# Index scores on 64 rows instead of 128, two heads side by side, issued between the token blocks of a weight phase

## The reference, cut to what matters

```python
def dsa_attention(h, w_in, q_gain, k_gain, w_uv, w_out, rel_bias):
    topk = min(TOPK_MAX, S // 4)
    q, lat, qi, ki, wi = jnp.split(h @ w_in, [o1, o2, o3, o4], axis=-1)
    q = rms_norm(q.reshape(B, S, DSA_HEADS, DSA_LATENT), q_gain)
    k = rms_norm(lat, k_gain)
    vals = lat
    qi = qi.reshape(B, S, IDX_HEADS, IDX_DIM)
    wi = wi * (IDX_HEADS ** -0.5)
    # for each block of 128 queries at t:
        isc = relu(einsum('bqhd,bsd->bqhs', qi_block, ki))      # one key row for all 8 heads
        isc = einsum('bqhs,bqh->bqs', isc, wi_block)
        isc = where(key_pos <= t, isc, NEG_2)
        _, sel = top_k(isc, topk)
        # softmax attention of the 16 heads over the selected keys, with a bias by distance
```

## Time and profile before

| | |
|---|---|
| runs before | 2037.31, 2037.4, 2040.08 us; median 2037.4 us |
| profiled execution | 2039.25 us; span of its instructions 2037.5 us |
| the stretch from the first index score to the last copy before the attention | about 1405 to 1524 us of the span |
| ACT busy over the span | 560.5 us (28%) |
| POOL busy over the span | 1215.8 us (60%) |
| chain that ended last, by engine | PE 90%, DVE 6%, ACT 2% |

### The profile page before, as it was taken

The page is one execution under the profiler, slowest core; times in us unless marked ns, Lnnn a source line. Parts: engine busy times, 40 slices in busy tenths (PEclk is TensorE's granted clock), DMA queues, the critical chain, the costliest instruction groups (busy, mean ns, idle before and its releaser), DMA issues.

```text
span 2037.5 us, 26586 instructions
## 1 busy us (share of the span) xinstructions
PE 1952.1 (96%) x9256; PEld 1570.0 (77%) x9264; DVE 1071.3 (53%) x1655; ACT 560.5 (28%) x1107; POOL 1215.8 (60%) x683
## 2 busy tenths in 40 slices
PE   6989999999998899998999999999999999999999
PEld 4876788888887777786788888877776678888887
DVE  4366479787785704555434433143986554333422
ACT  3117220000114306563312111132446522121110
POOL 6660578887674565566566666646660058666664
PEclk9999999999998899999999999999999999999999
DMA  6440267776551131114233233213220013332231
GB/s 246 134 162 5 63 206 258 247 238 219 192 169 58 63 103 42 42 42 160 68 105 101 93 97 99 93 52 104 73 83 2 1 62 114 93 100 95 93 101 64
DMA packets 62181, 221.14 MB, mean 109 GB/s; under 512 B 6763, under 2 KB 7019, under 8 KB 61980
## 3 DMA queue, kind: packets, MB, share of 16 engines
q1 hardware_dynamic: 44928, 161.25, 24.7%
q10 hardware_dynamic: 17180, 58.92, 8.1%
HBM read 218.00 MB, written 2.14 MB: 108 GB/s over the span
## 4 chain that ended last, share of the span: by engine, by line
PE 90%; DVE 6%; ACT 2%; issue 1%; DMA 1%; POOL 0%; ACTq 0%; DVEq 0%; SPq 0%
PE bank L300 25%; PE bank L302 24%; PE bank L301 24%; PE bank L330 2%; PE bank L795 2%; PE bank L335 2%; PE bank L331 2%; PE bank L413 1%; DVE y L1643 1%; PE bank L618 1%; PE bank L754 1%; PE bank L630 1%; PE bank L805 1%; PE bank L643 1%; PE bank L1257 1%
## 5 line engine op out<-in xcount | busy, mean ns | idle before, releaser
L1111 POOL TENSOR_TENSOR w_lo<-raw,w_hi 128x1024 fp32r<-128x1024 f32 (+1 forms) x305 | 771.2, 2529 | 25.0
L300 PE MATMUL bank<-a_hi,w_hi 128*128 128x512 f32 x1960 | 767.0, 391 | 7.2 <-ACT big L1346 3.5
L302 PE MATMUL bank<-a_hi,w_lo 128*128 128x512 f32 x1960 | 764.6, 390 | 0.0
L301 PE MATMUL bank<-a_lo,w_hi 128*128 128x512 f32 x1960 | 764.6, 390 | 0.0
L1106 POOL TENSOR_SCALAR w_hi<-raw 128x1024 fp32r<-128x1024 f32 x299 | 351.2, 1175 | 587.2 <-PE bank L302 362.9
L300 PEld LDWEIGHTS bank<-a_hi,w_hi 128*128 128x128 f32 x1960 | 369.0, 188 | 85.8 <-ACT big L1346 4.8
L302 PEld LDWEIGHTS bank<-a_hi,w_lo 128*128 128x128 f32 x1960 | 369.1, 188 | 77.3
L301 PEld LDWEIGHTS bank<-a_lo,w_hi 128*128 128x128 f32 x1960 | 369.1, 188 | 76.3
L1643 DVE CUSTOM_DVE_ANT_0 y<-y,cond 128x1024 f32<-128x1024 f32 x96 | 221.7, 2347 | 3.3 <-DMA y<-in_ada 3.3
L1658 DVE SCALAR_TENSOR_TENSOR tmp<-bank,vecs,tmp 128x511 f32<-128x511 f32 x88 | 66.0, 750 | 262.7 <-ACT tmp L1364 262.7
L1364 ACT ACTIVATE tmp<-bank,vecs 128x512 f32<-128x512 f32 x88 | 68.7, 782 | 372.6 <-PE bank L302 364.7
(11 more groups left out here) (232 smaller groups left out, 2140.4 us busy)
## 6 DMA issues: line engine op xcount, KB each, us to landing
raw<-in_stream SPq DMA_DIRECT2D x299, 512.0 KB, 3.5
y<-in_ada ACTq DMA_DIRECT2D x96, 512.0 KB, 4.6
x<-in_x SPq DMA_DIRECT2D x4, 512.0 KB, 7.0
bias<-in_bias ACTq DMA_DIRECT2D x1, 2048.0 KB, 14.1
y<-rel_rows ACTq DMA_DIRECT2D x1, 2048.0 KB, 8.8
bias<-rel_rows ACTq DMA_DIRECT2D x1, 2048.0 KB, 17.4
out<-x SPq DMA_DIRECT2D x8, 256.0 KB, 2.0
cond<-in_c ACTq DMA_DIRECT2D x1, 512.0 KB, 9.2
```

The lines of the kernel that those rows point to most:

```text
L300: pe.matmul(o, lhs_hi, rhs_hi, start=start, stop=False, **kw)
L301: pe.matmul(o, lhs_hi, rhs_lo, start=False, stop=False, **kw)
L302: return pe.matmul(o, lhs_lo, rhs_hi, start=False, stop=stop, **kw)
L1111: m = pool.tensor_tensor(w_lo[:, s, part], raw[:, j, part], f32(w_hi[:, s, part]), ALU.subtract)
```

## The change

Three things are done at once. Each head's matmul contracts over its own 64 rows (`half(h)`), so that the zeroed halves of `tmp` and the two memsets that made them are gone; the two heads of a pair are issued one right behind the other, on the upper and lower 64 rows, into two banks. The unit of issue is now a pair (12 in all), and the pair waits once, for both relus of the pair before it. Pairs are issued inside the dq blocks 1 to 6, behind token tiles 1 and 3 of each. Last, ACT's queue is rearranged to suit: relus 0 to 11, the copies of group 0, relus 12 to 15, and then two relus behind each token tile of squares.

```diff
-            def index_scores(n):
-                i, h = 1 + n // IDX_HEADS, n % IDX_HEADS
-                cols = P * (i + 1)
-                if n == 0:
+            def index_scores(pair):
+                if pair == 0:
                     pe.wait_ge(*freed("ki", 1))
-                    pe.wait_ge(index_init, 8)
+                    pe.wait_ge(index_init, 6)
                     pe.wait_ge(wi_taken, 1)
-                if n >= 2:
-                    pe.wait_ge(relu_ready, n - 1)
-                pe.matmul(bank[(4, 6)[n % 2]][:, 0:cols], big[:, 16 + h // 2, i * P:(i + 1) * P], tmp[:, 2 + h % 2, 0:cols],
-                          start=True, stop=True).then_inc(index_ready, 1)
+                else:
+                    pe.wait_ge(relu_ready, 2 * pair)
+                for n in (2 * pair, 2 * pair + 1):
+                    i, h = 1 + n // IDX_HEADS, n % IDX_HEADS
+                    cols = P * (i + 1)
+                    pe.matmul(bank[(4, 6)[n % 2]][:, 0:cols], big[half(h), 16 + h // 2, i * P:(i + 1) * P],
+                              tmp[half(h), 2 + h % 2, 0:cols], start=True, stop=True).then_inc(index_ready, 1)
...
-                m.then_inc(block_done, 1)
+                    if t == TT - 1:
+                        m.then_inc(block_done, 1)
+                    if t % 2 and i and 2 * (i - 1) + t // 2 < 3 * IDX_HEADS // 2:
+                        index_scores(2 * (i - 1) + t // 2)
...
-                for n in {0: range(6), 1: range(6, 12), 2: range(12, 18), 5: range(18, 24)}.get(i, ()):
-                    index_scores(n)
...
-            for n in range(18):
+            for n in range(12):
                 index_relu(n)
             token_copies(0)
+            for n in range(12, 16):
+                index_relu(n)
             a.wait_ge(lat_summed, 1)
             for t in range(TT):
                 token_squares(0, t)
-            for n in range(18, 3 * IDX_HEADS):
-                index_relu(n)
+                for n in range(16 + 2 * t, 18 + 2 * t):
+                    index_relu(n)
...
-            v.memset(tmp[64:P, 2, :], 0.0).then_inc(index_init, 1)
-            v.memset(tmp[0:64, 3, :], 0.0).then_inc(index_init, 1)
```

More of the change, by code:

```diff
@@ L1861, in index_add @@
                     v.wait_ge(wi_taken, 1)
-                    v.wait_ge(index_init, 8)
+                    v.wait_ge(index_init, 6)
                 else:
```

## The result

Over 18 runs each, the changed kernel took 2042.17 us (2040.68 to 2043.74) and the kernel before 2038.92 us: a ratio of 1.0016 with a 95% interval of 1.0009 to 1.0023, so 3.2 us slower. The prediction of 2036.9 us was wrong: the time lies above its range of 2033.2 to 2040.8, and half a microsecond less was forecast where three more came. It is still under the 0.2% that the prediction called the limit of telling; the interval from 18 runs each is clear of no change. One of the 18 runs before took 2478.31 us and is left out of the ratio, which compares fast runs alone.

The account below looks back on a forecast made before the run. PE sets the end with DVE's chain 1.40 us behind, so PE's saving is mostly waited away. DVE's terms, 1.9 + 1.3 - 2.8 - 0.7 - 0.2 = -0.5 us, on the median 2037.4 give 2036.9 us, range 2033.2 to 2040.8.

Parts of the forecast that it names:

- What bounds the stretch: Index-score stretch: PE sets the end, DVE runs 1.40 us behind; PE's 5.7 us saving is mostly waited away.
- The new wait of 1.5 us before block 4: PE before block 4: stands still for two relus, 0.88, and ACT's copy, 0.60, together 1.5 us.
- The wait of 4 us before block 8: PE before block 8: waits about 4 us for copies behind ACT's root of `q_inverse(0)`.
- A pair's cost: Index scores on PE: 0.75, 0.97 and 1.2 us for 256, 384 and 512 columns, 11.7 us in all.
- estimate of 0.15 for each change of mode: PE's tiling mode changes 24 times; at 0.15 us each PE would save 3.6 us instead of 7.2.
- Addition 8 +1.9: DVE's first top-k round: addition 8 waits for pair 4 and its relu, starting 1.9 us later.
- +1.3 up to `q_inverse(0)`: DVE from addition 8 to `q_inverse(0)`: the split of block 10 also falls here, costing 1.3 us, of 0 to 2.3.
- -2.8 and -0.7 behind it: DVE: block 10's split leaves `q_inverse(0)` and addition 20, saving 2.8 us; block 14's split costs `q_inverse(1)` 0.7 less.
- -0.2 at the end: Before line 1918: DVE's wait of 1.40 us goes, but the squares meet back-to-back splits; 0.2 us kept as gain.
- The end of the sum: DVE's terms from addition 8 to the stretch's end sum to -0.5 us, phases uncertain by 2 us either way.
- the rival on the clock: PE's clock halves around block 8 after its 4 us wait: +1.5 us, 2038.9 us; chance 12%.
- The third rival: Pairs' halves do not run side by side, or mode changes drain: pairs cost 1.1 to 1.8, 2042.7 us; chance 8%.

Follow-up runs that it names:

- e6: Changed kernel with GpSimd's splits of dq blocks 4 to 15 and the block behind them cut to one column: 2034.70 us, 0.9982 of the kernel before.
- e5: Kernel before with GpSimd's splits of dq blocks 4 to 15 and of uv cut to one column: 2038.60 us, ratio 1.0000.
- e3: Changed kernel with ACT's copies of group 1 in front of the root of `q_inverse(0)`: 2040.97 us, 1.0010 of the kernel before.
- e7: Changed kernel with every pair one place earlier, the first right behind the latents' sums: 2042.60 us, 1.0018 of the kernel before.
- e2: Changed kernel with scores over full 128 rows and zeroed halves, in the new places: 2038.16 us, 1.0002 of the kernel before.
- e1: Changed kernel with its 64-row pairs in the old four groups and ACT's relus in old order: 2043.81 us, 1.0026 of the kernel before.
- e11: Kernel before with ACT's copies of group 1 in front of the root of `q_inverse(0)`: 2044.59 us, ratio 1.0029.

## Why the prediction was wrong

- *What bounds the stretch*: right. PE's saving of 4.4 us up to block 7 is waited away before block 8, as the prediction said; e6 against e5 shows it is real, e3 that removing the wait alone gives the end nothing but one operation's phase.
- *The new wait of 1.5 us before block 4*: right (1.54), and right as to its cause. *The wait of 4 us before block 8*: right in cause, but the size, 3.91, is partly luck: PE came there 1.4 us later than forecast, and the copies it waits for 1.6 later.
- *A pair's cost*: 13.0 us instead of 11.7. Counted as the prediction did, from the pair's first row to the L301 behind it less a beat, a 256-column pair costs 1409.50 - 1408.54 - 0.23 = 0.73, as forecast (0.75); most of what was missing stands in front of the pair, which begins 0.32 us behind the matmul before it and not a beat, 0.23. Together a pair costs 0.17 us beyond its busy time. By the estimate of 0.15 for each change of mode it would have been 0.3. Before the waits PE saves 18.9 - 13.0 = 5.9 us, between the 7.2 of the forecast and the 3.6 of that estimate; behind the wait of 1.54 it is 4.4, not 5.7. On PE's own path this moved no time, since it waits before block 8; through addition 8 it did.
- *Addition 8 +1.9*: the mechanism was right (it waits for pair 4), the size was 2.55. Every pair in front of it cost 0.1 to 0.12 more than I put it at. Right in cause, but e7 shows that the term does not act alone.
- *+1.3 up to `q_inverse(0)`*: it measured +2.02, but the step behind it was wrong. I counted three splits before, those of blocks 7, 8 and 9, and a fourth after. The rows have four L1111 before (a first one at S + 23.0) and four after. It is not their number that made the difference: e2 has four as well and takes 34.1 us for this stretch, before 35.0, the changed kernel 37.0; e7, with five, 39.5.
- *-2.8 and -0.7 behind it*: -2.57 in place of -3.5. The splits have left the inverses, worth 2.5, and addition 20. This addition gave back 1.14 (2.77 to 1.63) and not 2.03, since POOL's scaling now stands beside it; the other three wide additions behind it gave back 1.0 that I had not counted. What I had not followed is where the splits went: one now stands over L1884, +2.05.
- *-0.2 at the end*: -0.19. The wait in front of line 1918 did not vanish, though (0.85 of 1.40 stayed), so the size was luck.
- *The end of the sum*: this is the step that failed, in two parts. The chain of DVE came out at +1.8 where I had -0.5: 0.65 of the difference from addition 8, 0.7 from the phase up to `q_inverse(0)`, 0.9 from the phase behind it. And the clock behind PE's last wait, a term of +1.6, was put at nothing. I read in the earlier trace rows that a wait of 2.5 us kept the clock at 1.00 and took that as safe for the last wait; the rival on the clock I placed at the wait before block 8 only. There the clock fell too, for seven matmuls, but nothing on the path followed, and e3 shows it. At the last wait every slow matmul is on the path. That rival, at +1.5, came near the size for another place.
- *The third rival* gave 2042.7 us, near to the time, but its cause isn't the right one: a 256-column pair costs 0.87 us, below its point of 1.1, and the two halves run side by side.

The phases alone missed by 1.6 us, within the 2 us that the range gave them; addition 8 and the clock came on top, and these had no share in the forecast's own range. One of the signs that the prediction had named against itself did show: mean durations of additions moved by more than 0.3 us, by -0.54 for the later ones over 512 keys and by +0.41 for the later ones over 384. With the clock's term in it the forecast would have been +1, and slower the likelier side. What remains open: why the clock fell behind some last waits and not behind others (below), and whether an order of splits exists that keeps e6's gain with the whole computation; no kernel here found it.

## What to carry to other kernels

Where operations of a chain on one engine are stretched when another engine's stand beside them, a change of timing elsewhere re-deals which operations are hit: cost both ends, follow every long operation to where it goes and not only from where it leaves, and expect several us of uncertainty: the same chain from addition 8 to the end of `q_inverse(2)` took 73.3 us in e2, 76.8 after, 77.3 before and 79.7 in e7, with the same operations on DVE. Time saved on an engine that does not set the end becomes a wait; look at what comes after the last such wait on the path, since there a fallen clock is paid in full. Before moving work, run the stretch once with the disturbing work taken out: it tells what bounds it.

## What the runs showed of the hardware

- *The length of PE's wait does not by itself tell whether its clock falls.* Last waits of 2.25 us (e7), 2.50 (before) and 2.50 (e2) were followed by 1.00; 2.27 (e6), 2.28 (e5), 2.36 (e1), 2.82 (e3), 2.83 (after) and 2.84 (e11) by 0.50. The fall cost 1.6 us in twelve matmuls each time in after, e3, e5 and e6, 1.5 in e1 and 2.4 in e11. In e6 the first matmul behind the wait was slow already (0.79 us), after the change only the second, in e3 only the fourth. What PE did before the wait doesn't decide it either: over the 16 us in front of it all nine have the same 73 matmuls with one idle stretch of 0.69 us, which ends 3.0 us before the wait. What decides stays open.
- *How much of a run is at half clock varies between runs of one kernel.* Of the 33 runs before on e5's chip, 19 have a mean granted clock of 0.982 and an average of 2037.9 us, seven 0.981 and 2039.8, six 0.980 and 2040.7; the 18 runs of the changed kernel lie between 0.977 and 0.981. So the slower runs of one kernel are those with more half clock. Where in a run it fell is known for the profiled execution alone. The Trainium skill ("TensorE: Matmul & The Clock Gate", What's actually happening) says that the number of slow matmuls varies between runs of one kernel; the means agree with that, without showing it for a single place.
- *A 64-row pair between three-pass matmuls.* Four instructions over 256, 384 and 512 columns are busy 0.70, 0.92 and 1.13 us, in all twelve places, and cost the stream 0.87, 1.08 and 1.30. Four full-row instructions cost 0.92, 1.34 and 1.77 (e2). So half rows save 0.05 us at 256 columns, but 0.47 at 512.
- *What POOL's operations stretch.* TENSOR_SCALAR is hit like the additions (L1884, 0.36 us alone, 2.59 beside L1111), the squares of line 1920 too (0.28 alone, 2.47). POOL's scaling does it as well: an addition over 512 keys beside L984 alone takes 1.63 us instead of 0.74. MAX8 over 384 keys has a mean of 556 ns before, 555 after and 555 in e7, whatever the phase. That the splits are the cause is shown by e5 and e6, where with one-column splits no addition up to `q_inverse(0)` is stretched; by what way they reach DVE, no run shows.
